# 24 activation tiles of the second half move between the gate maps, and two token chunks are added and normed ahead of the last 24 gathered rows

## The chip, the cores and the metric

One core of a Trainium2 chip runs the whole two-layer trunk in float32. The metric is the device time of one execution in microseconds (us); lower is better. Engines: TensorE (PE), VectorE (DVE), ScalarE (ACT), GpSimd (POOL) and SyncE (SP, which issues most DMAs).

## What is computed

The part of the reference that the change touches is the second sub-layer of each of the two layers, a retrieval over 16384 one-neuron experts, for 512 tokens of width 1024:

```python
def peer_mixer(h, wq, subkeys, u, v):
    q = (h @ wq).reshape(B, S, 8, 2, 128)
    scores = jnp.einsum('bshcd,hcnd->bshcn', q, subkeys)
    s_top, i_top = lax.top_k(scores, 16)
    ...                                   # the best 16 of the 16 x 16 sums per head
    gates = jax.nn.softmax(best, axis=-1)
    def chunk(args):                      # 128 tokens, 128 picked experts each
        a = jnp.einsum('cd,ced->ce', hh, jnp.take(u, ii, axis=0))
        act = jax.nn.gelu(a, approximate=False) * gg
        return jnp.einsum('ce,ced->cd', act, jnp.take(v, ii, axis=0))
x = x + gate2 * peer_mixer(...)           # then the next layer's norm, or the final norm
```

## The kernel before

The 512 tokens are four chunks of 128. Chunks 0 and 1 are *gathered*: per chunk and head one unit of 16 picks, 16 units in all; POOL fetches one expert row per token and pick by an indirect DMA (128 x 1024 floats, into a ring of 8 buffers), DVE takes the product with a row of `u` (L1481) or adds a weighted row of `v` into `peer_sum` (L1487). That is 512 such steps per layer, called rows here and numbered 0 to 511; `rows(l, first, end)` emits a range. Between them DVE selects the picks (`topk`, `topk_dense`).

Chunks 2 and 3 are *dense*: for them PE computes the activations of all 16384 experts, in 128 tiles of 128 experts, and ACT applies GELU. A tile of `u` (128 x 1024 floats) comes through one of four stream buffers; PE transposes it (`turn_u`, L575), ACT copies it out (`u_out`, L1037), PE multiplies it with the tokens (`act_tile`, L585), ACT writes the GELU of two tiles into `act_t` (`act_evac`, L969). `act_t` holds 64 tiles, so the layer goes in two halves. Which experts count is told by a *gate map* per token, a 128 x 128 matrix that PE makes as a product of two one-hot factors. There are 32 batches of 8 tokens (`gate_maps`): ACT and DVE make the factors (`p_batch` L1005 and L1009, `columns` L1496 and L1501), PE multiplies (L616), DVE multiplies the first half of the map into `act_t` (`gate_batch`, L1512), ACT copies the second half to a buffer (`keep_batch`, L1021), and SP writes it to memory. Factors and map banks are double buffered.

The order on PE in one layer: queries and the 64 activation tiles of half 0, the transposed picks (`turn_picks`, L603), the gate maps, the value products of half 0 (`value_tiles`, L632), the 64 activation tiles of half 1, the value products of half 1. DVE runs rows 175 to 191 between the batches of the gate maps and the rows from 192 on after them. The kept maps are read back and multiplied into half 1 of `act_t` between rows 368 to 399 and rows 432 to 463 (`kept_maps`, L1529). ACT computes the softmax and the GELU of each gathered unit (`unit_gates`) at fixed places of its own order. Behind row 511 `add_to_x` scales and adds the gathered chunks 0 and 1 to `x`, starts their norms, then does the same for the dense chunks 2 and 3 (L1598, L1601). Each engine executes in the order in which its instructions were written; semaphores are the only coupling.

## Time and profile before

| | us |
|---|---|
| median of 3 runs (lowest, highest) | 3776.0 (3771.5, 3783.2) |
| the profiled execution | 3776.3 |
| its span from first to last instruction | 3774.6 |
| PE, DVE, ACT, POOL busy | 3463.9, 2581.4, 994.8, 1357.6 |
| mixer of layer 0: gate maps | from 1072 to 1189 |
| value products half 0, activations half 1, value products half 1 | 1189 to 1409, to 1687, to 1907 |
| mixer of layer 1: the same four | from 2919, 3035, 3256, 3550 |

Busy times and shares are of the whole span. PE's busy share is not its share of peak, as matmuls are pipelined. The rows further down are of the profile's page, of its tables by stretch, of the lists of waits, of the chain of waits that ended last, and of the timeline. A stretch is named by its start and end in us from the start of the span.

### The profile page before, as it was taken

How to read it: one execution, taken by the hardware profiler on the slowest of the kernel's cores; microseconds unless marked ns; L12 is line 12 of the kernel's file. 1: busy time of each engine (PE TensorE's matmuls, PEld its weight loads, DVE VectorE, ACT ScalarE, POOL GpSimd, SP SyncE). 2: the span in 40 equal slices, each digit the busy share in tenths (PEclk: the TensorE clock that was granted, in tenths of full speed). 3: DMA queues.
4: the chain of work that ended last, by engine and by line, in shares of the span. 5: the costliest groups of instructions: out<-in, count | busy, mean ns of one | idle time of the engine just before them, and what ended most of it. 6: DMA issues, size and time to landing. Idle time of an engine off the chain costs nothing.

```text
span 3774.6 us, 46404 instructions
## 1 busy us (share of the span) xinstructions
PE 3463.9 (92%) x13798; PEld 2208.0 (58%) x13798; DVE 2581.4 (68%) x5509; ACT 994.8 (26%) x2173; POOL 1357.6 (36%) x1220
## 2 busy tenths in 40 slices
PE   6998998999947999999998989989997599999998
PEld 4555445777744448884445554457766544688643
DVE  5656115888898777777566641278998977687765
ACT  2333102323355003330023330123233720133200
POOL 0000001445332666676400000035444146666662
PEclk8999999999989999999999989999998999999999
DMA  5432124788766999999953222178888489999998
GB/s 226 159 106 78 72 85 174 289 334 309 293 206 206 404 405 401 374 388 399 409 195 106 103 81 106 52 263 338 311 306 291 151 317 395 406 387 349 389 401 327
DMA packets 275134, 999.40 MB, mean 265 GB/s; under 512 B 31481, under 2 KB 48377, under 8 KB 264449
## 3 DMA queue, kind: packets, MB, share of 16 engines
q0 software_dynamic: 153600, 553.72, 38.4%
q1 hardware_dynamic: 121346, 443.42, 31.4%
q8 instruction: 88, 1.44, 0.2%
q14 instruction: 100, 0.82, 0.1%
HBM read 971.85 MB, written 25.17 MB: 264 GB/s over the span
## 4 chain that ended last, share of the span: by engine, by line
PE 50%; DVE 22%; DMA 11%; issue 7%; DVEq 3%; POOL 3%; ACT 2%; another core or an unknown queue 0%; ACTq 0%; POOLq 0%; SPq 0%
PE ps L632 12%; PE ps L838 9%; PE ps L585 9%; DMA arena<-in_u_dram,idx 6%; DMA arena<-in_v_dram,idx 5%; DVE arena L1481 4%; DVE mod L1487 4%; PE ps L543 3%; PE ps L653 3%; PE ps L575 2%; POOL arena L1223 2%; PE ps L520 2%; DVE mod L1501 2%; PE ps L552 2%; PE ps L676 1%
## 5 line engine op out<-in xcount | busy, mean ns | idle before, releaser
L1223 POOL DMA_INDIRECT arena<-in_u_dram,idx x512 | 661.8, 1293 | 1031.1 <-issue 403.9
L585 PE MATMUL ps<-hT,mod 128*128 128x256 f32 x4096 | 929.0, 380 | 0.0
L632 PE MATMUL ps<-arena 128*128 128x512 f32 x1984 | 852.5, 592 | 3.4 <-DVE arena L1512 3.4
L585 PEld LDWEIGHTS ps<-hT,mod 128*128 128x128 f32 x4096 | 761.1, 191 | 93.6
L1223 POOL DMA_INDIRECT arena<-in_v_dram,idx x512 | 599.1, 1170 | 591.6 <-DVE mod L1487 289.9
L1481 DVE CUSTOM_DVE_ANT_0 arena<-arena 128x1024 f32<-128x1024 f32 x512 | 618.8, 1226 | 233.3 <-DMA arena<-in_u_dram,idx 213.2
L1487 DVE SCALAR_TENSOR_TENSOR mod<-arena,mod 128x1024 f32<-128x1024 f32 x512 | 657.3, 1284 | 161.1 <-DMA arena<-in_v_dram,idx 122.0
L632 PEld LDWEIGHTS ps<-arena 128*128 128x128 f32 x1984 | 376.7, 190 | 476.8 <-issue 471.6
L1037 ACT COPY mod<-ps 128x512 f32<-128x512 f32 x512 | 276.9, 590 | 519.6 <-PE ps L575 453.9
L575 PE MATMUL ps<-const,arena 128*128 128x128 f32 x2048 | 269.3, 274 | 21.2 <-ACT mod L1037 13.1
L575 PEld LDWEIGHTS ps<-const,arena 128*128 128x128 f32 x2048 | 237.6, 141 | 55.1 <-issue 33.7
L1646 DVE TENSOR_TENSOR arena<-arena,ps 128x512 f32<-128x512 f32 x32 | 22.0, 688 | 305.7 <-PE ps L838 305.7
L838 PE MATMUL ps<-hT,arena 128*128 128x512 f32 x512 | 227.2, 602 | 2.6 <-ACT arena L1152 2.6
L552 PE MATMUL ps<-hT,arena 128*128 128x512 f32 x512 | 226.6, 601 | 2.1 <-ACT hT L914 1.1
L1266 DVE SCALAR_TENSOR_TENSOR arena<-arena,c_act 128x256 f32<-128x256 f32 x384 | 184.7, 486 | 47.0 <-DMA arena<-in_ada_b_dram 17.6
L1202 POOL TENSOR_SCALAR_AFFINE_SELECT arena<-arena 128x128 f32<-128x128 f32 x32 | 10.1, 325 | 558.3 <-ACT arena L1107 558.3
L838 PEld LDWEIGHTS ps<-hT,arena 128*128 128x128 f32 x512 | 98.8, 194 | 127.6 <-issue 127.6
L969 ACT ACTIVATE arena<-ps 128x512 f32<-128x512 f32 x128 | 76.8, 600 | 363.6 <-PE ps L585 308.8
L552 PEld LDWEIGHTS ps<-hT,arena 128*128 128x128 f32 x512 | 98.7, 193 | 121.0 <-issue 120.2
L616 PE MATMUL ps<-cos_sin,mod 128*128 128x128 f32 x512 | 68.0, 288 | 97.4 <-issue 47.5
L543 PE MATMUL ps<-hT,arena 128*128 128x512 f32 x288 | 132.4, 615 | 2.6 <-ACT hT L914 1.5
L653 PEld LDWEIGHTS ps<-arena,hT 128*128 128x128 f32 x1024 | 118.0, 192 | 16.6 <-issue 15.6
(214 smaller groups left out, 3446.2 us busy)
## 6 DMA issues: line engine op xcount, KB each, us to landing
arena<-in_u_dram SPq DMA_DIRECT2D x256, 512.0 KB
arena<-in_v_dram SPq DMA_DIRECT2D x256, 512.0 KB
arena<-in_ada_w_dram SPq DMA_DIRECT2D x56, 1024.0 KB, 5.0
arena<-in_w_qkv_dram SPq DMA_DIRECT2D x48, 512.0 KB, 6.9
arena<-in_w_m_dram SPq DMA_DIRECT2D x16, 1536.0 KB, 6.2
arena<-in_w_q_dram SPq DMA_DIRECT2D x32, 576.0 KB
gate_scratch<-hT SPq DMA_DIRECT2D x64, 256.0 KB, 2.1
hT<-gate_scratch POOLq DMA_DIRECT2D x128, 128.0 KB
```

The lines of the kernel that those rows point to most:

```text
L543: last = pe.matmul(ps[:, bank, :], w_qkv[:, g, k, :], hT[:, k, :], start=(k == 0), stop=(k == KD - 1))
L552: last = pe.matmul(ps[:, c, :], q_w[:, c, k, :], hT[:, k, :], start=(k == 0), stop=(k == KD - 1))
L575: last = pe.transpose(ps[:, 4 + h, k * P:(k + 1) * P], stream[:, slot, kk * P:(kk + 1) * P], C(IDENT))
L585: last = pe.matmul(ps[:, 6 + tile // 2 % 2, tile % 2 * NT:(tile % 2 + 1) * NT], u_turned[:, tile % 2, k * P:(k + 1) * P], hT[:, k, DT0:SEQ ...
L632: last = pe.matmul(ps[:, 2 * c + n, :], act_t[:, e, c * P:(c + 1) * P], stream[:, slot, n * 512:(n + 1) * 512], start=(half == 0 and e == ...
L653: last = pe.matmul(ps[:, bank, c * P:(c + 1) * P], hT[:, k, c * P:(c + 1) * P], w_qkv[:, g, k, :], start=(k == 0), stop=(k == KD - 1))
L838: last = pe.matmul(ps[:, 4 * s + b, :], w_m[:, s, k0 + k, :], rhs[:, k, :], start=(k == 0), stop=(k == n - 1))
L1037: act.copy(u_turned[:, tile % 2, h * 512:(h + 1) * 512], ps[:, 4 + h, :]).then_inc(S["ut_ev"], 1)
L1223: pool.indirect_dma_start(out=ring[:, r % RING, :], out_offset=None, in_=table, in_offset=bass.IndirectOffsetOnAxis(ap=idx[:, j % 4, k:k + ...
L1266: last = dve.scalar_tensor_tensor(acc, ada_w[at % 3][:, k, :], c_act[:, k:k + 1], bias[:, cols] if k == 0 else acc, ALU.mult, ALU.add)
L1481: dve.tensor_tensor_reduce(row, row, h2[:, j % 2, :], 1.0, 0.0, ALU.mult, ALU.add, dots[:, j % 2, k:k + 1]).then_inc(S["row_used"], 1)
L1487: dve.scalar_tensor_tensor(total, row, coef[:, k:k + 1], total, ALU.mult, ALU.add).then_inc(S["row_used"], 1)
```

## The change

Activation tiles 0 to 23 of half 1 are computed earlier: four between the transposed picks and the first gate batch, and the other 20 behind 20 of the 32 gate batches. They use other PSUM banks (0 to 3) and other buffers for the transposed tile, since banks 4 to 7 and `p1` belong to the maps. `act_t` is still full with half 0 then, so ACT writes the GELU of two tiles into one of two small buffers, SP writes it to a scratch tensor in memory, and reads the 24 tiles back into `act_t` in six pieces of four tiles during the value products of half 0. The kept maps are applied at rows 320 and 376. Of ACT's gathered units, three sit between the later activation tiles, the others before or behind them. DVE adds and norms the dense chunks ahead of row 488, chunk 0 behind row 495 and chunk 1 behind row 511; the next layer's norm and transposes take the chunks in the order 2, 3, 0, 1. In the head loop DVE runs 16 rows instead of 10 ahead of the first selection, and 12 instead of 8 ahead of the last dense gates.

```diff
 KEPT = 4
+EARLY = 24
+FIRST = 4
+EARLY_AT = [-1] * FIRST + [b for b in range(NB) if (EARLY - FIRST) * (b + 1) // NB > (EARLY - FIRST) * b // NB]
+BACK = 4
+LATE_GATES = [28, 44, 62]
 ENDS = [0, 8, 16, 24, 32, 40, 44, 48]
 HEAD_ROWS = 21
 G_ROW = 175
 G_END = 192
-KEEP0 = 16 * 23
-KEEP1 = 16 * 27
+KEEP0 = 320
+KEEP1 = 376
+LAST_ROWS = UNITS * ROWS - TOPK
+KEY = 256.0
+ORDER = [[0, 1, 2, 3], [2, 3, 0, 1]]
...
+                def during_maps():
+
+                    for b in range(-1, NB):
+                        for t in tiles_at(b):
+                            if t == 0:
+                                after_u(HALF)
+                                load_u(l * TILES + HALF + STREAM, 0)
+                            if t + 1 < EARLY:
+                                after_u(HALF + t + 1)
+                                n = t + 1 + STREAM
+                                if n < EARLY:
+                                    load_u(l * TILES + HALF + n, n % STREAM)
+                                else:
+                                    load_v(l * TILES + n - EARLY, n % STREAM)
+                        if b >= 0 and b % 2 == 1:
+                            for r in (b - 1, b):
+                                sp.wait_ge(S["gs_done"], NB * l + r + 3)
+                                park()
+                                sp.dma_start(gate_dram[:, r:r + 1, :].rearrange("p a (b n) -> p (a b) n", b=2),
+                                             kept[r % KEPT]).then_inc(kept_out[r % KEPT], 16)
+                        for t in tiles_at(b):
+                            if t % 2 == 1:
+                                q = t // 2
+                                sp.wait_ge(S["a_ev"], HALF * l + HALF // 2 + q + 3)
+                                park()
+                                sp.dma_start(act_dram[:, 2 * q:2 * q + 2, :],
+                                             staged[q % 2].rearrange("p (a n) -> p a n", a=2)).then_inc(act_out[q % 2], 16)
...
+                def first_v():
+                    more_v(0, 1, 10)
+                    acts_back()
+                    for g in range(EARLY // BACK):
+                        sp.dma_start(act_t[:, BACK * g:BACK * (g + 1), :],
+                                     act_dram[:, BACK * g:BACK * (g + 1), :]).then_inc(S["act_back"], 16)
+                        more_v(0, 10 + g, 11 + g)
...
             def gate_maps(l):
 
-                with pe.Fori(0, NB // 2) as g:
-                    for s in range(2):
-                        b = NB * l + 2 * g + s
-                        pe.wait_ge(S["p_done"], b + 1)
-                        pe.wait_ge(S["q_done"], b + 1)
-                        pe.wait_ge(S["gm_done"], b + 1)
-                        pe.wait_ge(S["gs_done"], b + 1)
-                        for t in range(BATCH):
-                            last = pe.matmul(ps[:, G_BANK[s] + t // 4, t % 4 * P:(t % 4 + 1) * P],
-                                             p1[:, s, t * P:(t + 1) * P], q1[s][:, t * P:(t + 1) * P], start=True, stop=True)
-                        last.then_inc(S["g_done"], 1)
+                pe.wait_ge(S["qst_ev"], 2 * HEADS * (l + 1) + 2)
+                pe.wait_ge(S["sc_ev"], 2 * HEADS * (l + 1) + 2)
+                turn_u(l, 1, 0)
+                act_tiles(l, 1, 0, FIRST, EARLY)
+                for b in range(NB):
+                    s = b % 2
+                    pe.wait_ge(S["p_done"], NB * l + b + 1)
+                    pe.wait_ge(S["q_done"], NB * l + b + 1)
+                    pe.wait_ge(S["gm_done"], NB * l + b + 1)
+                    pe.wait_ge(S["gs_done"], NB * l + b + 1)
+                    for t in range(BATCH):
+                        last = pe.matmul(ps[:, G_BANK[s] + t // 4, t % 4 * P:(t % 4 + 1) * P],
+                                         p1[:, s, t * P:(t + 1) * P], q1[s][:, t * P:(t + 1) * P], start=True, stop=True)
+                    last.then_inc(S["g_done"], 1)
+                    for t in tiles_at(b):
+                        act_tiles(l, 1, t, t + 1, EARLY)
 
...
                 turn_picks(l)
                 gate_maps(l)
                 value_tiles(l, 0)
-                turn_u(l, 1, 0)
-                act_tiles(l, 1, 0, HALF)
+                turn_u(l, 1, EARLY)
+                act_tiles(l, 1, EARLY, HALF, HALF)
                 value_tiles(l, 1)
...
-                act.activation(act_t[:, 2 * pair:2 * pair + 2, :].rearrange("p a n -> p (a n)"), ps[:, 6 + pair % 2, :],
-                               ACT.Gelu).then_inc(S["a_ev"], 1)
+                early = half == 1 and 2 * pair < EARLY
+                to = staged[pair % 2] if early else act_t[:, 2 * pair:2 * pair + 2, :].rearrange("p a n -> p (a n)")
+                if early and pair >= 2:
+                    act.wait_ge(act_out[pair % 2], 16 * (EARLY // 4) * l + 16 * (pair // 2))
+                act.activation(to, ps[:, (2 if early else 6) + pair % 2, :], ACT.Gelu).then_inc(S["a_ev"], 1)
...
                 picks_out(l)
-                for b in range(NB):
-                    p_batch(l, b)
+                u_out(l, 1, 0)
+                for b in range(NB + 1):
+                    if b < NB:
+                        p_batch(l, b)
+                    for t in tiles_at(b - 1):
+                        act_tile(l, 1, t, EARLY)
                     if b >= 1:
                         keep_batch(l, b - 1)
-                keep_batch(l, NB - 1)
                 for j in range(5, 9):
                     unit_gates(l, j)
-                u_out(l, 1, 0)
-                for tile in range(HALF):
-                    if tile in (4, 19, 33, 48):
-                        unit_gates(l, 9 + (4, 19, 33, 48).index(tile))
-                    act_tile(l, 1, tile)
-                for j in range(13, UNITS):
+                u_out(l, 1, EARLY)
+                for tile in range(EARLY, HALF):
+                    if tile in LATE_GATES:
+                        unit_gates(l, 9 + LATE_GATES.index(tile))
+                    act_tile(l, 1, tile, HALF)
+                for j in range(9 + len(LATE_GATES), UNITS):
                     unit_gates(l, j)
...
@@ -1532,6 +1633,8 @@
 
                 dve.wait_ge(S["a_ev"], HALF * l + HALF // 2 + HALF // 4 * (part + 1) + 2)
                 park()
+                if part == 0:
+                    dve.wait_ge(S["act_back"], 16 * (EARLY // BACK) * (l + 1))
                 for r in range(NB):
...
                 for hd in range(HEADS - 1):
-                    rows(l, HEAD_ROWS * hd, HEAD_ROWS * hd + 10)
+                    middle = HEAD_ROWS * hd + (16 if hd == 0 else 10)
+                    rows(l, HEAD_ROWS * hd, middle)
                     topk_dense(l, hd, 0)
                     if hd == 0:
                         topk(l, 1)
-                    rows(l, HEAD_ROWS * hd + 10, HEAD_ROWS * hd + HEAD_ROWS)
+                    rows(l, middle, HEAD_ROWS * (hd + 1))
...
-                rows(l, HEAD_ROWS * (HEADS - 1), HEAD_ROWS * (HEADS - 1) + 8)
+                rows(l, HEAD_ROWS * (HEADS - 1), HEAD_ROWS * (HEADS - 1) + 12)
                 gates_dense(l, BLOCKS - 1).then_inc(S["pre_done"], 1)
-                rows(l, HEAD_ROWS * (HEADS - 1) + 8, G_ROW)
+                rows(l, HEAD_ROWS * (HEADS - 1) + 12, G_ROW)
...
@@ -1561,35 +1665,34 @@
                 kept_maps(l, 0, KEEP0)
                 rows(l, KEEP0 + NB, KEEP1)
                 kept_maps(l, 1, KEEP1)
-                rows(l, KEEP1 + NB, UNITS * ROWS)
+                rows(l, KEEP1 + NB, LAST_ROWS - TOPK // 2)
+                dense_to_x(l)
+                rows(l, LAST_ROWS - TOPK // 2, LAST_ROWS)
+                gathered_to_x(l, 0)
+                rows(l, LAST_ROWS, UNITS * ROWS)
+                gathered_to_x(l, 1)
...
-            def add_to_x(l):
+            def dense_to_x(l):
 
                 dve.wait_ge(S["x_back"], 128 * l + 128)
-                for c in range(GCH):
-                    dve.tensor_tensor(peer_sum[:, c, :], peer_sum[:, c, :], mod[:, GATE2, :], ALU.mult)
-                dve.drain()
-                for c in range(GCH):
-                    dve.tensor_tensor(x[:, c, :], x[:, c, :], peer_sum[:, c, :], ALU.add).then_inc(S["x_new"], 1)
-                for c in range(GCH):
-                    next_norm(l + 1, c)
...
+            def gathered_to_x(l, c):
+
+                dve.drain()
+                dve.tensor_tensor(peer_sum[:, c, :], peer_sum[:, c, :], mod[:, GATE2, :], ALU.mult)
+                dve.drain()
+                dve.tensor_tensor(x[:, c, :], x[:, c, :], peer_sum[:, c, :], ALU.add).then_inc(S["x_new"], 1)
+                dve.drain()
+                next_norm(l + 1, c)
```

PE, layer 0, from the transposed picks (`L603`, now `L681`) to the second half of the stage; `L575`/`L651` are transposes of a tile, `L585`/`L663` its products, `L616`/`L697` a gate batch, `L632` value products. Before (the pair of gate batches is a loop of 16 rounds):

```order
L585 MATMUL ps<-hT,mod 128x256 x16
L603 MATMUL ps<-const,g_row 128x128 x6
L608 UNCONDITIONAL_BRANCH
L608 ISA
L616 MATMUL ps<-cos_sin,mod 128x128 x8
L611 REGISTER_ALU
L616 MATMUL ps<-arena,mod 128x128 x8
L608 REGISTER_ALU
L608 COMPARE_AND_BRANCH
L632 MATMUL ps<-arena 128x512 x256
L575 MATMUL ps<-const,arena 128x128 x16
```

Of the changed kernel:

```order
L681 MATMUL ps<-const,g_row 128x128 x6
L651 MATMUL ps<-const,arena 128x128 x16
L663 MATMUL ps<-hT,mod 128x256 x8
...
L663 MATMUL ps<-hT,g_row 128x256 x8
L697 MATMUL ps<-cos_sin,mod 128x128 x8
L697 MATMUL ps<-arena,mod 128x128 x8
L651 MATMUL ps<-const,arena 128x128 x8
L663 MATMUL ps<-hT,mod 128x256 x8
L697 MATMUL ps<-cos_sin,mod 128x128 x8
```

Four tiles now stand between the picks and the first batch, and one behind 20 of the batches; the loop is written out.

DVE, end of layer 0, from the last 16 rows (`L1487`, now `L1588`) on; `L1587`/`L1712` scale a gathered chunk, `L1590`/`L1714` add it to `x`, `L1598` and `L1601` (`L1701`, `L1704`) do so for a dense one. Before:

```order
L1487 SCALAR_TENSOR_TENSOR mod<-arena,mod 128x1024 x16
L1587 TENSOR_TENSOR mod<-mod 128x1024 x2
L1590 TENSOR_TENSOR x_res<-x_res,mod 128x1024 x2
L1290 SCALAR_TENSOR_TENSOR mod<-mod,g_row 128x1024
L1276 TENSOR_SCALAR newton<-ss 128x1
L1277 TENSOR_TENSOR newton<-root 128x1
L1279 TENSOR_TENSOR newton<-newton 128x1
L1281 TENSOR_SCALAR newton<-newton 128x1
```

Of the changed kernel:

```order
L1588 SCALAR_TENSOR_TENSOR mod<-arena,mod 128x1024 x8
L1701 TENSOR_TENSOR arena<-ps,mod 128x1024
L1704 TENSOR_TENSOR x_res<-x_res,arena 128x1024
L1701 TENSOR_TENSOR arena<-ps,mod 128x1024
L1704 TENSOR_TENSOR x_res<-x_res,arena 128x1024
L1391 SCALAR_TENSOR_TENSOR mod<-mod,g_row 128x1024
...
L1397 TENSOR_TENSOR arena<-arena,mod 128x1024
L1588 SCALAR_TENSOR_TENSOR mod<-arena,mod 128x1024 x8
L1712 TENSOR_TENSOR mod<-mod 128x1024
L1714 TENSOR_TENSOR x_res<-x_res,mod 128x1024
```

The dense chunks (`L1701`) now stand between two groups of 8 rows, chunk 0 (`L1712`) behind the second of them.

## Rows read from the trace of the kernel before

**Rows 1.** The profile's page: busy us, share, count; a stream tile's DMA.
```profile
PE 3463.9 (92%) x13798; PEld 2208.0 (58%) x13798; DVE 2581.4 (68%) x5509; ACT 994.8 (26%) x2173; POOL 1357.6 (36%) x1220
...
arena<-in_u_dram SPq DMA_DIRECT2D x256, 512.0 KB
```
**Rows 2.** Table by stretch: start:end length, busy us by engine, granted clock, DMA share, GB/s.
```profile
1054.00:1072.00 18.00, 0.00 (x0) 0.00 (x0) 16.68 (x18) 0.26 (x1) 13.82 (x13) 0.50 0.98 360
1072.00:1189.00 117.00, 66.61 (x513) 61.23 (x514) 113.82 (x251) 83.40 (x213) 19.18 (x17) 0.99 0.47 151
1189.00:1409.00 220.00, 220.00 (x517) 97.50 (x516) 159.08 (x286) 12.38 (x20) 133.90 (x100) 1.00 0.99 385
1260.00:1330.00 70.00, 70.00 (x164) 30.97 (x163) 51.86 (x103) 3.22 (x6) 44.76 (x34) 1.00 1.02 401
1409.00:1687.00 278.00, 276.20 (x1526) 245.05 (x1525) 216.74 (x366) 97.41 (x179) 186.35 (x167) 1.00 1.00 387
1687.00:1895.00 208.00, 208.00 (x491) 92.92 (x490) 134.12 (x189) 11.43 (x17) 115.32 (x111) 1.00 1.02 400
```
**Rows 3.** Waits of DVE, then of PE, in 1189 to 1900: us, times, longest.
```profile
DVE arena L1481 <- DMA arena<-in_u_dram,idx: 97.0, 114, 2.4
DVE mod L1487 <- DMA arena<-in_v_dram,idx: 57.3, 62, 1.9
...
PE ps L632 <- DVE arena L1512: 1.7, 1, 1.7
```
**Rows 4.** The chain that ended last: start, us, what. Value products, two tiles, layer 1.
```profile
1188.73 219.97 PE ps L632 x512
...
1437.67 3.46 PE ps L585 x16
1442.00 3.46 PE ps L585 x16
...
3035.37 219.97 PE ps L632 x512
```
**Rows 5.** Timeline of the ends of layer 0 and of layer 1: start, us, engine, operation.
```profile
1893.40 1.28 DVE L1487 SCALAR_TENSOR_TENSOR mod<-arena,mod 128x1024 f32<-128x1024 f32 x1 [0.44 <-DMA arena<-in_v_dram,idx]
...
1907.61 1.22 DVE L1598 TENSOR_TENSOR arena<-ps,mod 128x1024 f32<-128x1024 f32 x1
...
1908.90 1.23 DVE L1601 TENSOR_TENSOR x_res<-x_res,arena 128x1024 f32<-128x1024 f32 x1
...
1922.52 2.90 PE L543 MATMUL ps<-hT,arena 128*128 128x512 f32 x3 [0.77 <-ACT hT L914]
...
3750.27 1.28 DVE L1487 SCALAR_TENSOR_TENSOR mod<-arena,mod 128x1024 f32<-128x1024 f32 x1 [1.10 <-DMA arena<-in_v_dram,idx]
...
3755.34 1.06 ACT L908 ACTIVATE h_row<-x_res 128x1024 f32<-128x1024 f32 x1 [78.31 <-DVE x_res L1590]
```
**Rows 6.** Waits of PE in the stretch of the gate maps, 1072 to 1189.
```profile
PE ps L616 <- issue: 23.5, 1, 23.5
```
**Rows 7.** Timeline: first gate batch, a later one with ACT's work, a tile's GELU.
```profile
1072.05 3.46 PE L616 MATMUL ps<-cos_sin,mod 128*128 128x128 f32 x16 [23.52 <-issue]
...
1101.89 2.02 PE L616 MATMUL ps<-cos_sin,mod 128*128 128x128 f32 x16 [1.58 <-ACT mod L1009]
...
1102.58 0.59 ACT L1021 COPY hT<-ps 128x512 f32<-128x512 f32 x1 [1.36 <-DVE arena L1512]
1103.06 0.99 ACT L1005 ACTIVATE mod<-iota,h_row 128x128 f32<-128x128 f32 x3
...
1104.12 1.26 ACT L1009 ACTIVATE mod<-mod,h_row 128x128 f32<-128x128 f32 x3
...
1445.49 0.60 ACT L969 ACTIVATE arena<-ps 128x512 f32<-128x512 f32 x1 [2.82 <-PE ps L585]
```
**Rows 8.** Waits of DVE in 1020 to 1050, and in 3256 to 3550.
```profile
DVE arena L1450 <- ACT arena L981: 7.2, 1, 7.2
...
DVE arena L1529 <- ACT arena L969: 11.0, 1, 11.0
```

175 lines of the change are left out of this document (105 added, 70 removed).

## The prediction, made before the changed kernel was timed

> **What bounds the kernel now.** I read the busy line and the slices first [rows 1]. TensorE (PE) is busy 92% of the span, which invites the conclusion that moving PE work into a gap pays in full. The table by stretch [rows 2] tells more. In the mixer of layer 0, the stretch of the gate maps (1072 to 1189 us) has DVE busy 113.8 of 117 us, PE 66.6 of 117, and memory moves only 151 GB/s. From 1189 on the picture is reversed: PE is full, and memory moves 385, 387 and 400 GB/s with a DMA share of 0.99 to 1.02. The third view is the waits [rows 3]: from 1189 to 1900 DVE waits 97.0 + 57.3 us for gathered rows to land, while PE waits 1.7 us for DVE and has no DMA among its releasers. So two chains run side by side after the gate maps. The dense chain is PE: 220 us of value products, 64 activation tiles at a pitch of 4.33 us, another 220 us [rows 2, 4]; its products release DVE's dense chunks from 1907.6 on. The gather chain is DVE fed by GpSimd's indirect DMAs, 320 rows (192 to 511) that are paced by memory; its last row starts at 1893.4 and ends at 1894.7 [rows 5]. They end 13 us apart, so the later of the two decides, and a gain on one alone is cut off by the other. That is why the sum below follows both.
>
> **The change, part by part (layer 0; layer 1 where it differs).** Sizes: a streamed tile and a gathered step are 512 KB = 0.524 MB each [rows 1].
>
> *Ahead of the maps.* PE turns 5 tiles and multiplies 4 in the 23.5 us in which it waited for DVE's first columns [rows 6]: 4 x 4.33 + 0.87 (pitch less the 3.46 of the products) = 18.2 us, hidden with 5 us to spare. The granted clock in that gap is 0.50 (1.2 GHz), after 18 us with no PE work, and the first map batch takes 3.46 us where the later ones take 2.02 [rows 2, 7]. The Trainium skill (TensorE: Matmul & The Clock Gate, Part 1) says that an idle array is throttled and activity releases it; with tiles in the gap the first batch would be warm and 1.4 us shorter, which lies within my rounding. DVE puts four more rows ahead of its wait for ACT's exponentials of 7.2 us [rows 8], which is worth 7.2 us at most; but in 1054 to 1072 memory is already at a share of 0.98 [rows 2], and now five tiles stream into it, so the rows that DVE needs come later. I take 2 us gained per layer (bounds 0 and 7).
>
> *The gate maps.* Before, 32 batches take 1188.73 - 1072.05 = 116.7 us [rows 4, 7], or 3.6 us each, and DVE is the limit. Now PE does 32 batches of 2.02 us and 20 tiles of 4.33 us [rows 4, 7]: 64.6 + 86.6 = 151.2 us. That is more than DVE's 113.8, so PE becomes the limit here. Off this comes the drain of a batch's last product, about 0.27 us, that a following tile covers (20 x 0.27 = 5.4). On it comes ACT: behind an odd tile it runs GELU 0.60, the copy of the map 0.59, and the weights of the next batch 0.99 + 1.26 [rows 4, 7], 3.4 us, while PE has only its 2.02 us batch when no tile follows. That is so for five tiles (9, 11, 13, 19, 21): 5 x 1.4 = 7.0 us. Last, the GELU and the copy behind tile 23 before the value products: 1.7 us. Sum 154.5, so +37.8 us, and with the 2 us above the maps end 35.8 us later. DVE has the same 17 rows to do in this stretch, so its gather chain starts its last 320 rows 35.8 us later too. Bounds of the window: 144 (no ACT waits, drain always covered) to 178 (151.2 and the 27 us of rival (c)). Covers: the 20 tiles and 3.1 MB of results (24 x 128 x 256 floats) written add 13.6 MB to 151 GB/s x 117 us = 17.7 MB, 203 GB/s in 154 us, far below what memory gives later; if SP's queue held a tile behind its wait for a map copy, four buffers of 4.33 us stand against it.
>
> *After the maps, the dense chain.* 24 tiles less: -24 x 4.33 = -104 us; PE needs 613 us.
>
> *After the maps, the gather chain.* It is paced by memory, so what counts is bytes: 24 x 0.524 = 12.6 MB of stream gone, 3.1 MB of activations read back, net 9.4 MB. At 390 GB/s, the mean of the three stretches [rows 2], that is 24.1 us. Rows 192 to 511 took 706.0 us, now 681.9. The Trainium skill (DMA: Bandwidth & Descriptors, Bandwidth) gives about 358 GB/s as the HBM side's limit and 425 as its largest measured transfer; the trace with 385 to 401 stands above the first and under the second. By 358 the relief would be 26.3 us, by 425 22.1 us. Neither changes the sum, but a stage that moved faster overall is a rival below.
>
> *Dense chunks ahead of the last 24 rows.* By the rows, PE is done at 613 us after the maps and row 488 comes at about 640, so DVE does not wait for it. DVE then spends 2 x (1.22 + 1.23) + 1.22 for the gain + 2 norms of 3.9 = 13.9 us, and for chunk 0 at row 496 8.7 us (product and sum 2.5, ACT's square and root 1.9, root step 1.3, norm 2.5, starts) [rows 5]. The ring holds 8 rows, so only about 2 us of gathering goes on behind it: +20.6 in the row stream. In exchange, the tail from the last row to the next layer's first projection, 1922.5 - 1894.7 = 27.8 us [rows 5], shrinks to one chunk: 8.7 + transposes and two copies 2.8 = 11.5, so -16.3.
>
> *Layer 0:* +35.8 - 24.1 + 20.6 - 16.3 = +16.0 us.
>
> *Layer 1:* from 3035.4 the rows take 716.2 us to 3751.6, the tail 23.1 to the span's end [rows 4, 5]. Here DVE waits 11.0 us (2.5 in layer 0) at its first kept map for an activation [rows 8], since ACT's gates sit at tiles 4, 19, 33, 48 and ACT waits there for DVE. With the kept maps at rows 320 and 376 and gates at tiles 28, 44, 62, and rows at their pace of before (32 in about 67 us among value products, 64 among tiles, 72 with kept maps, as the timeline has them), I get in us after the maps: tile 28 at 237 us against row 288 at 220; tile 44 at 307 against row 320 at 287; tile 62 at 385 against row 352 at 360; all tiles at 393 against row 376 at 401. So these waits go: -8.5. Insertion 10.3 + 7.4 less 2 = +15.7 (no gain step, no shift), tail 10.5 instead of 23.1: -12.6. Layer 1: +35.8 - 24.1 - 8.5 + 15.7 - 12.6 = +6.3 us.
>
> **Sum.** 16.0 + 6.3 = +22 us on the profiled execution's own 3776.3 us (span 3774.6, 1.7 us around it): 3798 us. The median of the runs shown is 3776.0, so nothing has to be shifted.
>
> **Rivals.** (a) *Memory goes faster, faster kernel.* The stretch 1260 to 1330 moves 401 GB/s [rows 2] where the mean that I use is 390. If the gather stage ran at 401 throughout, its 275.3 - 9.4 = 265.9 MB per layer would take 663.1 us instead of 681.9: -38 us in both layers, 3760 us. For it: the last stretch of before moves 400 already. Against it: DVE's stops for selection and the refill behind the maps stay. It decides from 396 GB/s upward, where the 22 us are gone. (b) *The dense chain sets the end.* Then each layer gains 104 - 35.8 = 68 us: 3640. Against it: 154 us of DVE waits for rows; those bytes do not go away. (c) *ACT's order stretches the maps* further: ten odd tiles cost PE 2.7 us each, +27 us per layer less the 7 already in: 3838 us. For it: ACT was idle only because it waited for DVE, and its queue is strictly in order. (d) *It evens out:* a window of 145 us in place of 154.5 takes 19 us off, 3779 us, no measurable change.
>
> **Chances.** My forecast (3785 to 3812) 0.50, (a) 0.20, (b) 0.03, (c) 0.13, (d) 0.14. What a measurement of this kernel can tell from no change is 0.3%, 11 us. Faster: (a) and (b), 0.23. Same (3765 to 3787): (d) and a little of my own, 0.18. Slower: 0.59. The range for 8 in 10 goes from (a) with the maps at their lower bound (3760 less 2 x 10.5) to just under (c): 3744 to 3832.
>
> **What would show it.** Of the changed kernel: PE busy about 90% in the maps, stretch near 154 us, DVE waiting some 30 us there for PE; granted clock 1.00 before the first batch. After the maps about 680 us for 320 rows with 385 to 395 GB/s, PE idle at the end for 60 us or more while rows still land; a tail of 11 us. I am wrong if the maps take 130 us or less, if the rows of the last stage need less than 650 us, or if PE ends after DVE's rows.

## The result, and the profile after

The changed kernel takes 3800.5 us (median of 16 runs, 3786.4 to 3808.9) against 3778.2 us for the kernel before on the same chip (16 runs): ratio 1.0053, 95% interval 1.0038 to 1.0068. It is slower by about half a per cent. The forecast was 3798. The profiled execution of the changed kernel has a span of 3795.2 us, against 3774.6: +20.6, where the sum said +22.

The page of the changed kernel, busy time and share, is nearly that of [rows 1]:

```profile
span 3795.2 us, 45936 instructions
...
PE 3443.4 (91%) x13798; PEld 2202.7 (58%) x13798; DVE 2587.6 (68%) x5509; ACT 985.9 (26%) x2173; POOL 1329.8 (35%) x1220
```

PE is busy 20 us less than before and the kernel is 20 us longer. The page can't tell why. The table by stretch can (columns as in [rows 2]; the stretches are the maps, value products, tiles, value products, the end of the rows in layer 0):

```profile
1064.00:1219.00 155.00, 145.87 (x984) 136.16 (x984) 115.53 (x251) 104.82 (x260) 19.17 (x17) 0.99 0.64 209
1219.00:1439.00 220.00, 219.58 (x512) 97.44 (x513) 148.46 (x267) 13.06 (x21) 119.32 (x96) 1.00 0.97 385
1439.00:1612.00 173.00, 171.77 (x950) 152.44 (x949) 137.74 (x226) 61.82 (x114) 112.88 (x110) 1.00 0.99 384
1612.00:1832.00 220.00, 217.35 (x512) 96.82 (x511) 157.95 (x276) 13.12 (x20) 138.69 (x125) 1.00 1.02 400
1832.00:1928.00 96.00, 11.72 (x38) 6.99 (x36) 84.41 (x101) 9.95 (x20) 47.55 (x46) 0.55 0.74 283
```

The maps' stretch was 117 us with DVE 113.82 busy and is 155 us with PE 145.87 busy, DVE 115.53: the limit changed hands. In the next three stretches memory moves what it moved before, 384 to 400 GB/s. In the last one PE has 11.72 us of work in 96, while DVE still works off rows.

The waits of DVE, then of PE, in the maps of layer 0 (us, times, longest), and the same two for the end of the layer:

```profile
DVE arena L1613 <- PE ps L697: 35.9, 23, 3.8
...
PE ps L697 <- ACT mod L1105: 8.3, 6, 1.6
PE ps L697 <- issue: 4.7, 1, 4.7
...
PE ps L587 <- DVE arena L1397: 91.6, 4, 44.5
```

DVE now waits 35.9 us for gate batches, 23 times; in 19 of them a tile's transposes and products stand directly ahead of the batch. After its last product PE waits 91.6 us for normed chunks. The timeline of PE shows both ends of the row stage (start, us, then the idle time before in brackets):

```profile
1063.86 3.36 PE L697 MATMUL ps<-cos_sin,mod 128*128 128x128 f32 x16 [4.71 <-issue]
...
1219.42 2.81 PE L716 MATMUL ps<-arena 128*128 128x512 f32 x6 [1.21 <-ACT hT L1117]
...
1828.96 8.85 PE L727 MATMUL ps<-arena 128*128 128x512 f32 x20 [1.15 <-DMA arena<-in_v_dram]
1882.35 1.97 PE L587 MATMUL ps<-const,arena 128*128 128x128 f32 x8 [44.54 <-DVE arena L1397]
...
1935.35 1.97 PE L587 MATMUL ps<-const,arena 128*128 128x128 f32 x8 [28.57 <-DVE arena L1397]
1938.08 7.42 PE L618 MATMUL ps<-hT,arena 128*128 128x512 f32 x10 [0.77 <-ACT hT L999]
```

First batch to first value product: 155.6 us (1188.73 - 1072.05 = 116.7 in [rows 4, 7]). The next layer's first projection starts at 1938.08 instead of 1922.52 [rows 5], 15.6 us later. DVE's timeline has the inserts (the first chunk's product, the first row behind it, chunk 0 and the first row behind that, and the sum behind the last row):

```profile
1872.44 1.23 DVE L1701 TENSOR_TENSOR arena<-ps,mod 128x1024 f32<-128x1024 f32 x1 [0.17 <-issue]
...
1885.69 10.92 DVE L1588 SCALAR_TENSOR_TENSOR mod<-arena,mod 128x1024 f32<-128x1024 f32 x8
1896.75 1.23 DVE L1712 TENSOR_TENSOR mod<-mod 128x1024 f32<-128x1024 f32 x1
...
1905.21 21.94 DVE L1588 SCALAR_TENSOR_TENSOR mod<-arena,mod 128x1024 f32<-128x1024 f32 x16
1927.30 1.23 DVE L1712 TENSOR_TENSOR mod<-mod 128x1024 f32<-128x1024 f32 x1
```

The dense insert holds the rows for 1885.69 - 1872.27 = 13.4 us, chunk 0 for 8.6. The last row ends at 1927.15, the tail to the projection is 10.9 us.

### The profile page after: what moved, and what is told of

Its sections match the earlier page's. It is cut to its first block, busy times and chain, and to the rows that moved or that the text cites. A ratio compares the mean times of both kernels' runs of the same rounds, so it can differ in the third digit from the quotient of the medians.

```text
span 3795.2 us, 45936 instructions
## 1 busy us (share of the span) xinstructions
PE 3443.4 (91%) x13798; PEld 2202.7 (58%) x13798; DVE 2587.6 (68%) x5509; ACT 985.9 (26%) x2173; POOL 1329.8 (35%) x1220
## 4 chain that ended last, share of the span: by engine, by line
PE 38%; DVE 21%; DMA 17%; issue 12%; POOL 5%; DVEq 4%; ACT 2%; ACTq 0%; POOLq 0%; SPq 0%
DMA arena<-in_u_dram,idx 14%; PE ps L922 9%; PE ps L663 8%; DVE mod L1588 5%; POOL arena L1324 4%; PE ps L618 4%; DVE arena L1582 3%; PE ps L737 3%; DMA arena<-in_v_dram,idx 3%; PE ps L697 3%; PE ps L651 2%; PE ps L595 2%; PE ps L760 1%; DVE arena L1480 1%; POOL hT L1313 1%
## 5 line engine op out<-in xcount | busy, mean ns | idle before, releaser
L1324 POOL DMA_INDIRECT arena<-in_u_dram,idx x512 | 643.4, 1257 | 1097.9 <-issue 393.5
L663 PE MATMUL ps<-hT,mod 128*128 128x256 f32 x3712 | 841.5, 380 | 1.1 <-ACT mod L1135 1.1
L1324 POOL DMA_INDIRECT arena<-in_v_dram,idx x512 | 589.5, 1151 | 627.3 <-DVE mod L1588 283.4
L1588 DVE SCALAR_TENSOR_TENSOR mod<-arena,mod 128x1024 f32<-128x1024 f32 x512 | 657.4, 1284 | 120.7 <-DMA arena<-in_v_dram,idx 86.8
L663 PEld LDWEIGHTS ps<-hT,mod 128*128 128x128 f32 x3712 | 689.4, 191 | 86.0 <-ACT mod L1135 1.9
L1135 ACT COPY mod<-ps 128x512 f32<-128x512 f32 x464 | 248.4, 589 | 460.2 <-PE ps L651 459.9
L651 PE MATMUL ps<-const,arena 128*128 128x128 f32 x2048 | 267.0, 274 | 12.1 <-ACT mod L1135 11.5
L651 PEld LDWEIGHTS ps<-const,arena 128*128 128x128 f32 x2048 | 237.0, 141 | 38.2 <-issue 19.6
L587 PE MATMUL ps<-const,arena 128*128 128x128 f32 x128 | 26.0, 370 | 121.9 <-DVE arena L1397 121.9
```

Source lines behind the costliest of these rows:

```text
L651: last = pe.transpose(ps[:, bank + h, k * P:(k + 1) * P], stream[:, slot, kk * P:(kk + 1) * P], C(IDENT))
L663: last = pe.matmul(ps[:, (2 if early else 6) + tile // 2 % 2, tile % 2 * NT:(tile % 2 + 1) * NT], turned[:, k * P:(k + 1) * P], hT[:, k, D ...
L1135: act.copy(turned[:, h * 512:(h + 1) * 512], ps[:, (0 if early else 4) + h, :]).then_inc(S["ut_ev"], 1)
L1324: pool.indirect_dma_start(out=ring[:, r % RING, :], out_offset=None, in_=table, in_offset=bass.IndirectOffsetOnAxis(ap=idx[:, j % 4, k:k + ...
L1588: dve.scalar_tensor_tensor(total, row, coef[:, k:k + 1], total, ALU.mult, ALU.add).then_inc(S["row_used"], 1)
```

## The experiments

Each was timed beside the kernel before, and the ratios compare with that. An interval of 95% follows each ratio. The times themselves come from several chips, on which the kernel before took 3775 to 3779 us, so small differences between two versions are read from the ratios. "Row" means a gathered step of DVE, 0 to 511 in each layer.

**1. Fewer tiles among the maps.**

```
-EARLY = 24
-LATE_GATES = [28, 44, 62]
-KEEP0 = 320
-KEEP1 = 376
+EARLY = 16
+LATE_GATES = [22, 36, 54]
+KEEP0 = 336
+KEEP1 = 400
```

> The changed kernel with 16 early tiles instead of 24, so 12 of them stand between the gate batches instead of 20; kept maps at rows 336 and 400, ACT's gates at tiles 22, 36 and 54, so that they still come at their old places in the rows. Theory (the gate maps are lengthened by PE once its tiles no longer fit beside DVE, and the stage behind is paced by memory): PE needs 32 x 2.02 + 12 x 4.33 = 117 us in the maps, about DVE's own 114, so the window is 120 to 132 us instead of 155.6; rows 192 to 511 gain 6.3 MB, two thirds of the 20 us that the 24 tiles gave. Per layer about 27 us less in the maps and 7 more behind them than in the changed kernel: 3760 us, below the kernel before. Rival (the loss is the cost of moving a tile, by its scratch traffic and ACT work, so it is in proportion to the tiles moved): two thirds of the loss stay, 3793 us.

Measured: 3799.95 us, ratio 1.0052 (1.0038 to 1.0067), the same as with 24. The theory that the maps take the larger of PE's and DVE's work fell: it had 120 to 132 us for them and they took 143.7. The rival's 3793 us is a ratio of 1.0045 and lies inside the interval, so the rival is not refuted; PE waits 14.2 us for ACT's weights here, which is a part of what it names. The stretch of the maps and the waits of PE in it:

```profile
1064.00:1208.00 144.00, 119.75 (x792) 111.79 (x792) 115.61 (x254) 96.10 (x240) 19.31 (x18) 0.94 0.58 188
...
PE ps L697 <- ACT mod L1105: 14.2, 10, 2.1
PE ps L697 <- DVE mod L1602: 8.5, 3, 3.1
```

PE and DVE have 120 and 116 us of work and need 144: neither is full. A batch goes round DVE's columns, ACT's weights, PE's products, DVE's product and back into two buffers. My reading is that a tile of 4.3 us in front of one batch delays that batch by more than its neighbours can catch up; a deeper set of buffers, which would tell, was not tried. A small part is the clock: at a granted 0.94, PE's busy time was 119.75 us for work that the theory priced at 117. Twelve tiles between batches cost 143.7 - 116.7 = 27 us, 2.3 us each; twenty cost 38.9, 1.9 each. On the mean a tile costs more when there are fewer. And the 12 us won in the maps were lost behind them: rows 192 to 511 took 706.5 us instead of 695.7 in layer 0, with 8 more tiles beside them. (The traced execution took 3810.8 us, the longest of its six and 11 us above their median, so the loss behind the maps may be a little less as a rule.)

**2. Fewer bytes beside the rows of the changed kernel.** Half the columns of the 40 later tiles are not loaded, 10.5 MB a layer.

```
-                        load_u(l * TILES + HALF + EARLY + s, s)
-                    more_u(HALF + EARLY + STREAM, HALF - EARLY - STREAM)
+                        load_u(l * TILES + HALF + EARLY + s, s, True)
+                    more_u(HALF + EARLY + STREAM, HALF - EARLY - STREAM, True)
```

> The changed kernel, with only the first 512 of 1024 columns loaded for the 40 u tiles behind the maps (the other half of each buffer stays old data): 10.5 MB less per layer, all instructions on PE, ACT and DVE the same. Theory (behind the maps the rows are paced by memory and PE has slack): rows 192 to 511 end 22 to 27 us earlier per layer, 3750 us. Rival (behind the maps the end is set by the order on PE and ACT): no change, 3800 us.

Measured: 3785.35 us, ratio 1.0026 (1.0011 to 1.0040): 15 us less than the changed kernel by the medians and 10 by the ratios, for two layers, in place of 50. Nearer to the rival. Rows 192 to 511 ended 8.0 and 6.5 us earlier after the first value product, where 22 to 27 were expected. The stretch of the tiles in this version, then DVE's waits for rows there:

```profile
1437.00:1610.00 173.00, 171.77 (x950) 152.47 (x949) 146.65 (x237) 61.84 (x114) 117.97 (x120) 1.00 0.94 351
...
DVE arena L1584 <- DMA arena<-in_u_dram,idx: 14.8, 27, 1.5
DVE mod L1590 <- DMA arena<-in_v_dram,idx: 1.8, 5, 0.9
```

Memory fell from 384 to 351 GB/s instead of moving the rows as much faster. DVE is busy 146.65 of 173 us and waits 16.6 us for rows; in the changed kernel it waited 27. The queues' view of the same stretch, in 40 slices, shows how the bytes were missed; the first line is the changed kernel in 1439 to 1612, the second this version:

```profile
GB/s 409 408 406 408 409 407 410 409 410 406 407 409 404 400 398 233 152 370 335 390 402 400 401 398 398 401 397 404 399 400 401 397 411 408 409 243 335 366 418 410
...
GB/s 400 172 300 327 408 407 407 405 407 399 405 393 387 141 102 239 308 400 380 383 354 386 368 375 378 355 393 362 320 387 400 261 203 296 401 406 411 411 406 400
```

In the changed kernel memory stands near 400 and falls below 300 twice. In this version it falls to between 102 and 300 three times, each time as one of DVE's selections ends (at 1440, 1497 and 1573 us in its timeline), and it stays under 400 for a good part of the rest. With less stream beside them the 8 rows that fit ahead are soon there, and nothing more can be fetched while DVE does something else. So memory is the first limit, but DVE with its stops is close behind it, and freed bytes are worth no more than the gap. (That the ring's depth sets it is my reading; another depth was not tried.) What was won is then cashed at a lower price: 395 us after the first value product this version is at row 376 and the changed kernel at row 369, and those 7 rows saved about 8 us at the end, where a row takes 1.3 to 1.4 us.

**3. Fewer bytes beside the rows of the kernel before.** The same edit to all 64 tiles of the second half, 16.8 MB a layer left out.

```
-                        load_u(l * TILES + HALF * half + s, s)
+                        load_u(l * TILES + HALF * half + s, s, half == 1)
...
-                more_u(HALF + STREAM, HALF - STREAM)
+                more_u(HALF + STREAM, HALF - STREAM, True)
```

> The kernel before, with only half of the columns loaded for the 64 u tiles of half 1: 16.8 MB less per layer. Theory (before the change PE's dense chain ends 13 us behind the rows, and the tail waits for it): the rows end 30 to 43 us earlier but PE does not, so layer 0 gains nothing and layer 1 at most the 9 us that ACT waited for DVE: 3768 to 3778 us. Rival (the rows alone set the end before, too): 35 to 43 us per layer, 3700 us.

Measured: 3756.8 us, ratio 0.9942 (0.9925 to 0.9958): some 20 us faster, a little more than the theory said and far from 3700. 43 us of memory time a layer shortened rows 192 to 511 by 8.6 us in layer 0 (693.9 to 685.3) and by 18.2 in layer 1 (703.9 to 685.7). DVE's waits in 1430 to 1900 name the next limits:

```profile
DVE mod L1489 <- DMA arena<-in_v_dram,idx: 45.5, 47, 1.5
DVE arena L1483 <- DMA arena<-in_u_dram,idx: 45.0, 61, 2.1
DVE arena L1531 <- ACT arena L971: 15.3, 2, 13.5
```

The rows got ahead and then stood 15.3 us at the kept maps, 19.8 in layer 1, which need an activation tile that PE had not reached: row 352 came 12.5 us earlier after the first value product than before, row 376 only 2.7. From the first value product to the next projection layer 0 gained 3 us, and layer 1 gained 11 to its end, much as the theory had it (nothing, and 9 at most): PE's chain ends this kernel's layers. So this run does not price the bytes alone; part of what they bought was lost to the dense chain.

**4. Rows into the maps of the changed kernel.** Since DVE waits 35.9 us there, 16 more rows go in.

```
-G_END = 192
+G_END = 208
@@ ACT, behind the weights of batch 0
+                    if b == 0:
+                        unit_gates(l, 5)
@@ ACT, behind the maps
-                for j in range(5, 9):
+                for j in range(6, 9):
```

with the late gates at tiles 28, 40 and 54 and the kept maps from rows 336 and 400.

> The changed kernel, with rows 192 to 207 and the selection behind row 192 also done by DVE between the gate batches (33 rows in the maps instead of 17), ACT's gates of unit 5 moved ahead of the maps, kept maps at rows 336 and 400, gates at tiles 28, 40, 54. Theory (in the lengthened maps DVE idles 36 us and memory is half idle, which is where the gain went): 16 x 1.37 + 8.9 = 31 us of DVE work fit into those 36, the maps grow by 0 to 8 us, and rows 208 to 511 start with the value products: 22 to 33 us less per layer, 3734 to 3756 us. Rival (the maps take as long as DVE's and ACT's chain needs in each batch, so more DVE work lengthens them): 3795 to 3805 us.

Measured: 3784.2 us, ratio 1.0020 (1.0010 to 1.0030), faster than the changed kernel by 0.33%, a third of the least that the theory had (44 us in two layers). The maps took 166.7 us (+11), and row 288 came at 1397 instead of 1444. Then the lead melted: at row 320 DVE waited for ACT.

```profile
DVE arena L1565 <- ACT arena L1071: 6.2, 1, 6.2
DVE arena L1568 <- ACT arena L1082: 1.4, 1, 1.4
```

**5. That wait mended.**

```
-                for j in range(6, 9):
+                for j in range(6, 10):
-LATE_GATES = [28, 40, 54]
+LATE_GATES = [34, 47, 62]
```

> As the version with 16 more gathered rows among the gate maps (3784 us), with one thing mended: the gates of unit 9 are computed ahead of the late activation tiles and those of units 10 to 12 at tiles 34, 47 and 62, so that DVE's row 320 does not wait for them (7.6 us in layer 0) and PE's tiles not for ACT behind DVE (9.6 us). Theory, that these waits gave back most of the 47 us lead of row 288: 10 to 20 us less, 3765 to 3774 us. Rival, that the lead is cashed in at DVE's pace of 1.35 us a row anyway, since memory is the limit only while PE's tiles stream: within 4 us of 3784.

Measured: 3773.6 us, ratio 0.9995 (0.9983 to 1.0008). That is 0.25% under the version of experiment 4, at the edge of what the theory had. In 1440 to 1640 DVE now waits for nothing but rows. The traced execution took 3791.6 us, the longest of its twelve, so the gain in time is read from the ratio and not from its timeline. Sixteen rows and one place of a gate pay back what the change had cost.

**6. The same rows in the kernel before, without tiles.**

```
-G_END = 192
+G_END = 208
```

with the gates of unit 5 behind batch 0, late gates at tiles 3, 16, 31, 46, kept maps from rows 384 and 448.

> The kernel before (no tiles among the maps), with 16 more gathered rows among its gate maps (G_END 208), the gates of unit 5 behind the first batch, the kept maps 16 rows later and the late gates 1 to 3 tiles earlier. DVE is the limit of the maps there, so 16 rows of 1.3 us lengthen them by 21 us. Theory (after the maps a row costs 2.2 us since memory paces it, and memory moves only 151 GB/s in the maps): 16 x 2.2 = 35 us come back, net -14 us in each layer, about 3750 us. Rival (in before the dense chain follows 13 us behind the rows, 1907.6 against 1894.7, and it starts 21 us later): 21 us slower in each layer, 3810 us or more.

Measured: 3834.4 us, ratio 1.0154 (1.0133 to 1.0174): the rival, with more than its 21 us a layer. The maps' stretch, and DVE's wait at the end of layer 0:

```profile
1063.00:1211.00 148.00, 85.26 (x512) 78.64 (x512) 142.58 (x303) 82.47 (x211) 40.84 (x33) 0.77 0.55 174
...
DVE arena L1600 <- PE ps L643: 25.3, 2, 20.9
```

The maps took 148.6 us, +32 for 16 rows, with DVE full. 29 of the 32 are DVE's own work (142.58 - 113.82): the forecast of 21 had the rows, and left out the selection behind row 192, for which experiment 4 had set 8.9. PE started its 719 us of dense work at 1212.0 instead of 1188.7, and here PE's chain ends the layer: DVE, done with its rows, waits 25.3 us for its products. The last row ended 7 us earlier than in [rows 5] and the next projection started 25 us later. In this kernel a lead of the rows bought nothing; in the changed one a lead of PE buys nothing.

**7. Dense chunks last in the changed kernel.**

```
-                rows(l, KEEP1 + NB, LAST_ROWS - TOPK // 2)
+                rows(l, KEEP1 + NB, UNITS * ROWS)
                 dense_to_x(l)
-                rows(l, LAST_ROWS - TOPK // 2, LAST_ROWS)
                 gathered_to_x(l, 0)
-                rows(l, LAST_ROWS, UNITS * ROWS)
                 gathered_to_x(l, 1)
```

> The changed kernel, only with the dense chunks added and normed after row 511 instead of ahead of row 488, and gathered chunk 0 at the end too. My step: the inserts cost the row stream 22.0 us in layer 0 and shorten the tail by 16.9 us, so undoing them changes each layer by about -5 (layer 0) and -3 us (layer 1): 3792 to 3800 us. Rival: PE and memory stand idle then, so DVE's dense work is hidden there behind rows still landing (the ring of 8 rows and what memory delivers meanwhile) and early dense chunks are a real gain: then this version is slower, 3815 to 3828 us.

Measured: 3804.1 us, ratio 1.0074 (1.0058 to 1.0089), 0.2% above the changed kernel's ratio, with overlapping intervals. The traces say even more plainly that the insert is neutral: from row 480 to the next projection it is 77 us in both (1859 to 1936.26 here, 1861 to 1938.08 there), in layer 1 to the end 71 in both. The time of the inserts (22.0 us) and of the tail they save (32.5 - 10.9 = 21.6) cancel. I expected this version to gain 5 and 3 us; it gained nothing, and the rival's 15 us or more are not there either.

**8. The rows among the heads alone**, in the kernel before:

```
-                    rows(l, HEAD_ROWS * hd, HEAD_ROWS * hd + 10)
+                    middle = HEAD_ROWS * hd + (16 if hd == 0 else 10)
+                    rows(l, HEAD_ROWS * hd, middle)
```

and 12 in place of 8 ahead of the last dense gates.

> The kernel before, with only the changed kernel's spread of rows over the heads: 16 rows (not 10) ahead of the second selection of head 0, and 12 (not 8) ahead of the last dense gates. In the changed kernel the first map batch of layer 0 came 8.2 us earlier where I had forecast 2. If this edit is what brought it, the first batch here starts near 1064 us and the kernel is 6 to 8 us faster, about 3768 us. Rival: the earlier start comes from PE having tiles in the gap or from the loads ahead of it; then the first batch stays near 1072 us and the time is 3776 within 3 us.

Measured: 3766.6 us, ratio 0.9979 (0.9962 to 0.9996), about 8 us faster, with an interval of 2 to 14. But the early first batch (1060.23) is no proof of it, since the version of experiment 6, with the old spread, starts at 1063.41 too: that start varies by 8 us between executions. The traced execution took 3754.6 us, the shortest of its twelve and 12 us under their median, so what it gains is in part chance. What the trace shows is who ends the layer: the value products began at 1177.72, 11 us earlier than in [rows 4], and the next projection at 1910.21, 12 us earlier than in [rows 5], so all but 1 us of the lead was there before the value products. The chain that ended last is PE there (start, us, what):

```profile
1677.97 206.00 PE ps L632 x480
1883.97 13.75 PE ps L643 x32
```

**9. The old spread in the changed kernel**, the same edit undone there.

> The changed kernel with the rows among the heads as in before (10 and 8 in place of 16 and 12). Alone, the new spread took the kernel before from 3779 to 3767 us. If that gain is in the changed kernel too, this one is 8 to 12 us slower than the changed kernel, 3808 to 3812 us, and the tiles among the maps with the early dense chunks cost 30 us or more. Rival: the rows' chain gets nothing from it here, since it ends in DVE and memory work and not in PE: within 4 us of 3800.

Measured: 3805.3 us, ratio 1.0074 (1.0060 to 1.0089): 0.2% above the changed kernel, between theory and rival. From row 0 to row 480 both need 1233 and 1230 us in the two layers to within 1 us, so the trace shows no gain. Its first batch came at 1062.72, as early as with the new spread. I take the spread to be worth 2 to 14 us in the kernel before and leave open whether it is worth anything in the changed one, where the two intervals overlap.

**10. Both chains shortened alike.** 12 tiles early, the 16 rows, the mended gates, and gathered chunks ahead of the dense ones again.

```
-EARLY = 24
+EARLY = 12
-LATE_GATES = [28, 44, 62]
+LATE_GATES = [19, 36, 53]
-G_END = 192
+G_END = 208
-ORDER = [[0, 1, 2, 3], [2, 3, 0, 1]]
+ORDER = [[0, 1, 2, 3], [0, 1, 2, 3]]
-KEEP0 = 320
-KEEP1 = 376
+KEEP0 = 352
+KEEP1 = 416
...
```

> Both chains shortened by like amounts: 12 tiles early in place of 24, 16 more gathered rows among the maps (G_END 208), the gates of units 9 to 12 placed ahead of and at tiles 19, 36 and 53, kept maps from rows 352 and 416, and at the end the order of before (all rows, gathered chunks, then dense chunks). The maps take 116.7 + 21 (16 rows at 1.3) + about 14 for the part of 8 tiles between batches that is not hidden = 152. PE: +35 - 12 x 4.33 = 17 us earlier than in before at its end; rows: +35 - 16 x 2.2 - about 8 for the tiles' bytes = 8 us earlier. With the head rows' 5 us, 13 us less per layer: 3750 us (3740 to 3762). Rival, that tiles and rows in one window add up (as 11 us were added for 16 rows beside 20 tiles) and the lead of the rows is lost while they share memory with the tiles: 3776 or more.

Measured: 3779.1 us, ratio 1.0007 (0.9991 to 1.0023). A miss of the theory. The time is the rival's (3776 or more), but the trace shows a cause that neither had. The maps took 156.9 us, close to the 152 expected. DVE then stood at the first kept map:

```profile
DVE arena L1624 <- ACT arena L1058: 17.4, 1, 17.4
```

and 14.6 us in layer 1. I had put the kept maps earlier by the place of the tile and forgotten that the rows come earlier too.

**11. The same with 8 tiles** (kept maps from 360 and 424, gates at tiles 19, 33, 49).

> As the version with 12 tiles early, with 8 (late gates at tiles 19, 33, 49, kept maps from 360 and 424). Maps about 116.7 + 21 + 8 = 146; PE ends +29 - 35 = 6 us earlier than in before, rows +29 - 35 - 5 = 11 us earlier: PE decides, 6 + 5 us less per layer, 3755 us; that is 0 to 10 us above the version with 12. Rival, rows decide in both: then the shorter maps win and this version is 5 us faster than the one with 12.

Measured: 3785.2 us, ratio 1.0027 (1.0013 to 1.0041), 0.2% above the version with 12, which fits the theory's difference, though the intervals overlap and in the traces the two layers differ in sign (next projection at 1924.12 here and 1930.36 with 12, the end at 3780.4 and 3779.4). That PE decides is not shown. The time itself was missed for the same reason. The maps took 151.4 us, 5.5 less than with 12; DVE waited 14.5 us at the same place, and 16.1 in layer 1.

**12. The kept maps later.**

```
-KEEP0 = 352
-KEEP1 = 416
+KEEP0 = 372
+KEEP1 = 424
```

> The version with 12 tiles early, only with the kept maps 20 and 8 rows later (from rows 372 and 424 in place of 352 and 416). In that version DVE stood 17.4 us in layer 0 and 14.6 us in layer 1 at the first kept map, for an activation tile that PE had not reached, and memory fell to 356 GB/s meanwhile, since only 8 rows can be gathered ahead. Theory, these waits are a loss in full, because DVE and memory, not PE, end the layer there (PE waits 35 us for DVE at the end): 3779 - 32 + about 8 for what the rows lose again beside the tiles, 3750 to 3760 us. Rival, that a lead gained while tiles stream is given back as before: 3770 us or more.

Measured: 3764.1 us, ratio 0.9973 (0.9959 to 0.9987), 13 to 15 us under experiment 10, or about half of the 32 us of waits, and 4 us above the theory's band. The wait is gone, and the two chains meet. PE's timeline, last products and first transposes and projection:

```profile
1874.00 8.85 PE L727 MATMUL ps<-arena 128*128 128x512 f32 x20 [1.25 <-DMA arena<-in_v_dram]
1892.46 1.97 PE L587 MATMUL ps<-const,arena 128*128 128x128 f32 x8 [9.61 <-DVE arena L1391]
...
1910.70 16.77 PE L618 MATMUL ps<-hT,arena 128*128 128x512 f32 x32 [0.77 <-ACT hT L999]
```

PE ends at 1882.85, the last row at about 1882.5, the next projection starts at 1910.70 (1922.52 before, 1938.08 changed). It beats both kernels, 0.27% under the one before and 0.8% under the changed one; experiment 8, at 0.9979, does as well within the intervals with a far smaller edit.

## Why the prediction was right, and where it was lucky

**The maps (+37.8).** Measured +38.9 in layer 0 and +37.6 in layer 1 (2930.54 to 3084.81, 154.3 us). PE was the limit with 20 tiles (145.87 us busy in 155), and the term for ACT was near: PE waited 8.3 us for ACT's weights, where 7.0 stood in the sum. The bound of 144 that I gave as "no ACT waits" rests on a rule that fell in experiment 1: with 12 tiles between the batches, PE's own 64.6 + 52 us = 117 is hardly more than DVE's 114, and the maps took 144. The number held because 20 tiles fill PE.

**The start (-2).** Measured -8.2 in layer 0 and -3.7 in layer 1 (from the layer's own start). Experiment 6, with the old spread and no tiles in the gap, had its first batch at 1063.41 too, so most of the 8 us can be variation between executions. That the first batch would run at full clock was wrong in layer 0: it took 3.36 us behind 4.71 us of idle time, with a granted clock of 1.00 among the tiles before that (1040 to 1060). In layer 1 it was right:

```profile
2930.54 2.02 PE L697 MATMUL ps<-cos_sin,mod 128*128 128x128 f32 x16 [0.63 <-issue]
```

The Trainium skill (TensorE: Matmul & The Clock Gate, Part 1) has activity release the throttle and idleness bring it back. The two batches agree with both halves of that; The forecast counted on the first and had nothing for the gap between the last tile and the batch.

**The relief of the rows (-24.1).** Measured -20.3 (from 1219.42 to 1927.15, less 22.0 of inserts, 685.7 against 706.0); in layer 1 the whole rest of the layer is 28.8 us shorter, where the terms give 29.5: rows -32.6 for -32.6, inserts +17.0 for +15.7, tail -13.2 for -12.6. The wait of 11.0 us at the kept map is gone there, but the wait for ACT's gates grew from 2.5 to 5.5 us. The size is right, and the reason, "what counts is bytes", holds for this change and is no general price. Experiments 2 and 3 took 27 and 43 us of memory time out of a layer; the rows ended 6.5 to 8 us earlier in the first, 8.6 and 18.2 in the second, where a wait at the kept maps took a part. The relief in the changed kernel does not lie beside the tiles, where memory still moves 384 GB/s: at row 464 it is 621.0 us past its first value product where the kernel before was at 597.6, 23 us behind. It lies in the last 96 us, when PE's stream has ended: rows come there at DVE's own pace (8 rows in 10.92 us above, 1.37 each) instead of 2.2 us on the mean of the row stage of before (706.0 / 320). The queues' view of 1840 to 1872 shows it, with nothing but the gather in flight (packets, MB, mean):

```profile
DMA packets 3600, 13.11 MB, mean 410 GB/s; under 512 B 400, under 2 KB 400, under 8 KB 3600
```

13.11 MB are 25 gathered steps of 0.524 MB in 32 us, 1.28 us each. Memory's pace and DVE's are the same there within 0.1 us. In these runs, then, bytes moved ahead of the rows paid nearly in full, by 20.3 us of 24.1, and bytes taken away beside the tiles paid a fifth to two fifths.

**Rival (a), 401 GB/s throughout:** the stretches ran at 385, 384 and 400. It did not come. (The lower end of the range rests on it and has a slip: 3760 less 2 x 10.5 is 3739, not 3744. The measured time is far from either.)

**The inserts and the tail (+20.6 - 16.3).** Measured +22.0 and -16.9 in layer 0. Against the order of before, this costs 5 us, where the forecast had 4. Experiment 7 shows that it is not the order that costs them: with the dense chunks last, the changed kernel is no faster. The tail was 27.8 us before, when the gathered chunks were normed while PE still worked, and 32.5 in experiment 7, where PE is done early and there is nothing left to hide them behind.

**The dense chain (PE done at 613 us after the maps, row 488 at about 640).** Measured 618 (1828.96 + 8.85 for the last products, less 1219.42) and 653 (the insert starts at 1872.27). Rival (b), 3640 us, had no support: PE's 104 us of saved tiles became 91.6 us of waiting. Experiments 3 and 6 add which way round it goes: in before the two chains end 13 us apart, with PE last, and rows that ended 9 and 7 us earlier brought 3 us in the one and nothing in the other. The change brought PE's last product forward by 71 us (1837.8 against 1908.7) and put the last row back by 32 (1927.15 against 1894.7), of which the shorter tail returns 17.

**Rivals (c) and (d):** ACT cost 8.3 us, not 27, and the maps were no shorter than 154.

Carried to the sum: -8.2 + 38.9 - 20.3 + 22.0 - 16.9 = +15.5 in layer 0 (forecast +16.0), +5.1 in layer 1 (+6.3). With the -2 of the forecast in place of the -8.2, layer 0 would have come to +21.7: the sum fitted to 1.4 us partly because an error of 6 us in the start, which can be chance, went against errors of 1 to 4 us in the other terms. That closeness is luck; the mechanism of each term is not.

## What to carry to other kernels

Where two chains end a stage within a few us of each other, filling one engine's gap pays nothing until the other chain is shortened by as much: read from the waits at the stage's end which of them waits for which, and price a move on both. A double-buffered ring of three engines need not take the larger of their loads: here the work put between its steps cost 1.9 to 2.3 us for each piece of 4.3, about half its own length. And each lead won needs its followers moved with it: in experiments 3, 4 and 10 a gate or a kept map at a place that no longer fitted made DVE wait 8 to 20 us.

## What the runs showed of the hardware

- The granted clock of a stretch can fall although the work in it is the same. The 32 gate batches ran at 0.99 with 66.6 us of PE in 117 [rows 2], and at 0.77 with 85.26 in 148 in experiment 6: batches took 2.02 us or up to 3.75, the two levels of 2.4 and 1.2 GHz:

```profile
1197.51 2.02 PE L616 MATMUL ps<-arena,mod 128*128 128x128 f32 x16 [0.78 <-issue]
...
1206.52 3.75 PE L616 MATMUL ps<-arena,mod 128*128 128x128 f32 x16 [2.01 <-issue]
```

It cost that kernel about 19 us of PE time in the maps; DVE was the limit there, so this is not 19 us of the kernel's. The idle time just before a batch does not settle it: the slow batch above stood behind 2.01 us, and in the kernel before a batch at full clock stood behind 3.06:

```profile
1080.36 2.02 PE L616 MATMUL ps<-cos_sin,mod 128*128 128x128 f32 x16 [3.06 <-DVE mod L1501]
```

- With one core at work, gathered rows alone moved 410 GB/s (above), and rows and tiles together 384 to 401 in the stretches shown. The Trainium skill (DMA: Bandwidth & Descriptors, Bandwidth) lets the HBM side bind at about 358 for such transfers, and also gives that figure as each core's part when both cores of a pair stream. No stretch with full queues here stays under it, and the section's 425 for its largest transfer, with the neighbour core idle, is the nearer figure.
